# Conditioning products summed on VectorE, and RWKV's first pair with its inputs loaded at once

## The reference

```python
for l in range(DEPTH):                     # DEPTH = 2
    cond = jax.nn.silu(c) @ w_ada[l] + b_ada[l]
    shift, scale, gate_raw = jnp.split(cond, 3, axis=-1)
    h = x * (1.0 + scale[:, None]) + shift[:, None]
    proj = h @ w_in[l]
    ...
    a = jax.nn.sigmoid(rw_a0[l] + a_down @ rw_a_up[l])
    kk = heads(k * rw_k_k[l], RW_HEAD)
    kk = kk / jnp.maximum(jnp.sqrt(jnp.sum(jnp.square(kk), -1, keepdims=True)), L2_EPS)
    ...
    x = layer_norm(DN_ALPHA * x + (1.0 + gate_raw[:, None]) * out, ln_g[l], ln_b[l])
...
mod = silu_c @ w_ada[l] + b_ada[l]         # second model, 6 * 1024 wide
mod_c = silu_cc @ w_ada[l] + b_ada[l]      # the same weights, another vector
```

## Time and profile before

| | us |
|---|---|
| Median of 3 runs (lowest to highest) | 5123.26 (5112.72 to 5138.3) |
| Profiled execution, its time | 5130.85 |
| Its span, first to last instruction | 5129.1 |
| Mean granted clock of TensorE | 0.907 |
| Busy: TensorE, VectorE, ACT, GpSimd | 4337.1, 1568.6, 1108.3, 751.6 |
| Last operation of `modulation` starts | 62.16 |
| First projection matmul of layer 0 (L400) | 87.51 |
| Last copy of layer 0's projection (L340) | 608.63 |

### The profile page before, as it was taken

How to read it: one execution, slowest core, us unless ns; L and a number is a source line. 1 busy time by engine, 2 the same in 40 slices (tenths; PEclk the granted TensorE clock), 3 DMA queues, 4 the chain that set the end, 5 groups by cost and what they waited for, 6 DMA issues and landing times. The chain is left out here.

```text
span 5129.1 us, 74458 instructions
## 1 busy us (share of the span) xinstructions
PE 4337.1 (85%) x28872; PEld 2808.1 (55%) x28872; DVE 1568.6 (31%) x2365; ACT 1108.3 (22%) x1499; POOL 751.6 (15%) x555
## 2 busy tenths in 40 slices
PE   6999867887998899757779996888778999999962
PEld 3666655665665688646656664453434444444431
DVE  2000265443232100645542412452221111111127
ACT  1000233322122111333321213340201111111110
POOL 1111101001222322000102220000050000000014
PEclk8999977878999899878879998999779999999985
DMA  4334312231221222210002221000107999999966
...
DMA packets 170080, 715.25 MB, mean 139 GB/s; under 512 B 26882, under 2 KB 28675, under 8 KB 134019
## 3 DMA queue, kind: packets, MB, share of 16 engines
...
## 5 line engine op out<-in xcount | busy, mean ns | idle before, releaser
L400 PE MATMUL ps<-s_proj_hS,s_proj_wS 128*128 128x512 f32 x3216 | 762.3, 398 | 62.2 <-POOL s_proj_wS L312 62.2
L400 PEld LDWEIGHTS ps<-s_proj_hS,s_proj_wS 128*128 128x128 f32 x3216 | 605.6, 189 | 223.6 <-ACT s_proj_wS L361 63.1
L1806 PE MATMUL ps<-s_mix_hS,s_mix_wS 128*128 128x512 f32 x1536 | 394.9, 413 | 40.1 <-POOL s_mix_wS L1665 35.5
L1806 PEld LDWEIGHTS ps<-s_mix_hS,s_mix_wS 128*128 128x128 f32 x1536 | 291.4, 190 | 134.9 <-issue 67.5
L2720 PE MATMUL ps<-s_exp_gu,keep_hT 128*128 128x512 f32 x736 | 340.1, 605 | 14.8 <-DMA s_exp_gu<-in_w_gu_dram 12.9
L2704 PE MATMUL ps<-s_exp_wd,s_exp_aT 128*128 128x512 f32 x736 | 332.9, 595 | 1.9 <-ACT s_exp_aT L2630 1.9
L2725 PE MATMUL ps<-s_exp_gu,keep_hT 128*128 128x512 f32 x736 | 330.9, 592 | 0.0
L1665 POOL TENSOR_TENSOR s_mix_wS<-s_mix_w,s_mix_wS 128x1024 fp32r<-128x1024 f32 x96 | 230.7, 2404 | 582.3 <-ACT s_mix_wS L1674 582.3
L312 POOL TENSOR_TENSOR s_proj_wS<-s_proj_w,s_proj_wS 128x1024 fp32r<-128x1024 f32 x67 | 162.8, 2433 | 690.1 <-ACT s_proj_wS L361 690.0
L340 DVE COPY s_proj_o<-ps 128x512 f32<-128x512 f32 x66 | 45.6, 692 | 707.4 <-PE ps L400 707.4
L2670 DVE TENSOR_TENSOR s_exp_sg<-s_exp_sg,ps 128x256 f32<-128x256 f32 x92 | 38.7, 421 | 660.1 <-ACT s_exp_sg L2651 660.1
...
## 6 DMA issues: line engine op xcount, KB each, us to landing
...
```

Of the source, the lines that this page charges most:

```text
L400: mm = pe.matmul(k.ps[:, 6 + half if last else 2 * b + half, :], wS[:, b, x, t, :], hS[:, y, t, half * HALF:(half + 1) * HALF], start=(t = ...
L1806: mm = pe.matmul(k.ps[:, bank, :], wS[:, b, u, x, :], src[:, v, x, :], start=(x == 0 and u + v == 0), stop=(x == KT - 1 and u == 1))
```

## The change

`modulation` makes only slabs 0 to 15. Layer 0's gate joins the slabs that are made during layer 0's projection. These are made in another way: for 8 slabs at a time (a round of the projection), tiles that hold the c-th 128 inputs of all 8 slabs are loaded, c = 0 to 7, in four buffers within `k.mix`; VectorE multiplies each by one scalar per partition (`k.silu`) and adds it to a running sum, one sum for layers 0 and 1 (`ONE`, rounds 0 to 3), two for the second model (`TWO`, rounds 4 to 9). The tiles are worked in the first two steps of a round. At the head of the next round TensorE sums over the partitions: 8 matmuls for each sum, the sum as the stationary operand and one column of ones as the moving one. The products before were for three vectors in all slabs; now they are only for those that are used.

In `rwkv`, the first pair's key, query, low-rank weights come ahead of the masks, the masks have a semaphore of their own, decay, rate and norms go to banks 6, 4 and 2, and the three products stand one behind another.

```diff
     GRP = 4
-    NG = NADA1 // GRP
+    NS = 2 * KT
+    NG = NS // GRP
...
 
     nc, I = k.nc, k.I
     NB = 3
-    R1, R2 = 1, 9
-    NX = (2 * NADA1 + NADA2 - NADA1) // (NB * (R2 - R1))
+    ONE, TWO = (2 * KT, 4), (2 * NADA1, 6)
+    NWA = 4
...
+            acc, wa = k.mix[:, 0:2], k.mix[:, 2:2 + NWA]
+            ld_a = [s.sem(f"ld_a{x}") for x in range(NWA)]
+            acc_ready, ada_ready, ada_taken = [s.sem("acc_ready0"), s.sem("acc_ready1")], s.sem("ada_ready"), s.sem("ada_taken")
...
-            parts = [(0, 1, False), (1, 2, True), (2, R2, True), (R2, NR - 1, False), (NR - 1, NR, False)] if not l else \
-                [(0, 1, False), (1, NR - 1, False), (NR - 1, NR, False)]
-            for a, z, ada in parts:
-                if z == a + 1:
-                    for b in range(NB):
-                        yield a, b, ada
+            na, nb = ONE[1], ONE[1] + TWO[1]
+            parts = [(0, 1, ONE, None), (1, 2, ONE, ONE), (2, na, ONE, ONE), (na, na + 1, TWO, ONE), (na + 1, nb, TWO, TWO), (nb, NR, None, TWO)] if not l else \
+                [(0, 1, None, None), (1, NR - 1, None, None), (NR - 1, NR, None, None)]
...
-                            yield i, b, ada
+                            yield i, b, cur if b < 2 else None, old if b == 0 else None
...
+        def group(g, kind):
+
+            return (g - ONE[1], 2, TWO[0], range(1, 3)) if kind is TWO else (g, 1, ONE[0], range(0, 1))
...
-            for i, b, ada in steps(sp):
+            def tiles(i, b, cur):
+                g, nv, s0, vs = group(i, cur)
+                for c in range(4 * b, 4 * b + 4):
+                    wait(sp, acc_ready[0], i * KT + (c - NWA + 1))
+                    if nv == 2:
+                        wait(sp, acc_ready[1], g * KT + (c - NWA + 1))
+                    sp.dma_start(wa[:, c % NWA].rearrange("p (g n) -> p g n", g=KT),
+                                 I["w_ada"][bass.ds(g * KT + s0, KT), :, c, :].rearrange("g p n -> p g n")).then_inc(ld_a[c % NWA], 16)
+
+            late = []
+            for i, b, cur, old in steps(sp, unrolled=True):
                 n = i * NB + b
                 wait(sp, lo_ready, n - NB + 1)
                 src = I["v_down"] if isinstance(n, int) and n == NSCAN else I["w_in"][l, n]
                 sp.dma_start(w[:, b], src).then_inc(ld_w[b], 16)
-                if ada:
-                    m = n - R1 * NB
-                    wait(sp, ada_ready, m)
-                    for x in range(NX):
-                        sp.dma_start(wa[:, x], I["w_ada"][m * NX + (NADA1 + x)]).then_inc(ld_a[x], 16)
+                late.append((i, b, cur))
+                if len(late) > 2 and late[-3][2]:
+                    tiles(*late[-3])
...
                 wait(dve, st_o[b], i * 16, 16)
                 dve.tensor_copy(o[:, b, HALF:T], k.ps[:, 2 * b + 1, :]).then_inc(taken_v, 1)
-                m = n - R1 * NB
-                if ada and not (isinstance(m, int) and m == 0) or isinstance(n, int) and n == R2 * NB and not l:
-                    wait(dve, turned, m)
-                    dve.tensor_copy(k.cond[:, bass.ds((m - 1) * NX + NADA1, NX), :],
-                                    k.ps[:, 7, 0:3 * NX].rearrange("p (g v) -> p g v", g=NX)).then_inc(ada_taken, 1)
-                if ada:
-                    wait(dve, ada_ready, m + 1)
-                    dve.tensor_copy(row[:], k.ps[0:3, 6, 0:NX * P]).then_inc(row_ready, 1)
+                if old:
+                    g, nv, s0, vs = group(i - 1, old)
+                    wait(dve, ada_ready, i)
+                    dve.tensor_copy(k.cond[:, bass.ds(g * KT + s0, KT), vs[0]:vs[0] + nv],
+                                    k.ps[:, 7, 0:KT * nv].rearrange("p (v g) -> p g v", v=nv)).then_inc(ada_taken, 1)
+                if cur:
+                    g, nv, s0, vs = group(i, cur)
+                    for c in range(4 * b, 4 * b + 4):
+                        wait(dve, ld_a[c % NWA], i * 2 * 16 + (c // NWA + 1) * 16, 16)
+                        for v in range(nv):
+                            done, at = acc_ready[v], (g if v else i) * KT + c
+                            scale = k.silu[:, c, vs[v]:vs[v] + 1]
+                            if c:
+                                wait(dve, done, at)
+                                dve.scalar_tensor_tensor(acc[:, v], wa[:, c % NWA], scale, acc[:, v], ALU.mult, ALU.add).then_inc(done, 1)
+                            else:
+                                wait(dve, ada_ready, i)
+                                dve.tensor_scalar(acc[:, v], wa[:, 0], scale, None, ALU.mult).then_inc(done, 1)
...
-            for i, b, ada in steps(pe):
+            for i, b, cur, old in steps(pe):
                 n = i * NB + b
                 last = isinstance(n, int) and n == NSCAN
+                if old:
+                    g, nv, s0, vs = group(i - 1, old)
+                    wait(pe, acc_ready[0], i * KT)
+                    if nv == 2:
+                        wait(pe, acc_ready[1], g * KT + KT)
+                    wait(pe, ada_taken, i - 1)
+                    for v in range(nv):
+                        for x in range(KT):
+                            mm = pe.matmul(k.ps[:, 7, v * KT + x:v * KT + x + 1], acc[:, v, x * P:(x + 1) * P], k.ones[:, 0:1],
+                                           start=True, stop=True)
+                    mm.then_inc(ada_ready, 1)
                 wait(pe, hi_ready, n + 1)
                 wait(pe, lo_ready, n + 1)
...
         bones, lora, vup = s.sb("bones", [P, P]), s.sb("lora", [P, 2, P]), s.sb("vup", [32, 2, P])
         proj, vfirst = k.scratch["proj"], k.scratch["vfirst"]
 
+        def prep(q, x):
+
+            return 6 if q else {"decay": 6, "rate": 4, "residual": 2, "norms": 2}[x]
+
         def previous(n):
             return edge[:, n, 0:T]
 
...
+            sp.dma_start(par[:, :, 0:13], I["rw_par"][l]).then_inc(ld_par, 16)
             sp.dma_start(b, proj[CLOW]).then_inc(ld_low, 16)
-            sp.dma_start(par[:, :, 0:13], I["rw_par"][l]).then_inc(ld_par, 16)
+            sp.dma_start(e1, proj[CK]).then_inc(ld_k, 16)
+            sp.dma_start(lora[:, 0], I["rw_lora"][l, 0]).then_inc(ld_lora, 16)
+            if l:
+                sp.dma_start(vup[:, 0], I["v_up"][0]).then_inc(ld_lora, 16)
+            sp.dma_start(e2, proj[CR]).then_inc(ld_r, 16)
             sp.dma_start(pairs, I["pair_masks"][:, 0:1 + NLV, :]).then_inc(ld_pm, 16)
+            sp.wait_ge(low_in, 1)
+            sp.dma_start(b, proj[CV]).then_inc(ld_v, 16)
+            if l:
+                sp.dma_start(vf[:], vfirst[0]).then_inc(ld_vf, 16)
             for h in range(2):
-                sp.dma_start(mLN[rows(h)], I["causal_masks"][rows(h), :, rows(h)]).then_inc(ld_par, 16)
-                sp.dma_start(at_st[rows(h)], I["level_masks"][rows(h), 1:2 + NLV, rows(h)]).then_inc(ld_par, 16)
-            sp.wait_ge(low_in, 1)
-            inputs(0)
+                sp.dma_start(mLN[rows(h)], I["causal_masks"][rows(h), :, rows(h)]).then_inc(ld_mask, 16)
...
             act.activation(lo[0:HD, :], lo[0:HD, :], ACT.Tanh).then_inc(low_tanh, 1)
             key_part(0)
             query_part(0)
-            value_part(0)
             square(0)
             decay(0)
             rate(0)
+            value_part(0)
             residual(0)
             norm(0)
             exps(0)
...
-            dve.wait_ge(ld_par, 16 * NMASK)
+            dve.wait_ge(ld_par, 16)
...
+            dve.wait_ge(own, mine.n)
+
+            shift_key(0)
+            shift_query(0)
+            floor(0)
+            shift_value(0)
+            mix(0)
+            dve.wait_ge(shift_v, 1)
+            cumulate(0)
             for h in range(2):
                 dve.wait_ge(turn_m, 1)
                 mine.mark(dve.tensor_copy(at_ts[rows(h)], banks(k, 0)[rows(h), 0:(1 + NLV) * P]
                                           .rearrange("p (m n) -> p m n", n=P)[:, :, rows(h)]))
-            dve.wait_ge(own, mine.n)
-
-            shift_key(0)
-            shift_query(0)
-            shift_value(0)
-            floor(0)
-            mix(0)
-            dve.wait_ge(shift_v, 1)
-            cumulate(0)
...
+            dve.wait_ge(ld_mask, 16 * NMASK)
...
-                pe.wait_ge(ssm_ready, q + 1)
+                if q:
...
-                    pe.wait_ge(sig_a, q + 1)
...
-                pe.wait_ge(sig_w, q + 1)
+                wait(pe, sig_w, q + 1 if q else 0)
...
+            pe.wait_ge(low_tanh, 1)
+            pre_decay(0)
+            pre_rate(0)
+            key_norms(0)
             pe.wait_ge(ld_pm, 16)
             for n in range(1 + NLV):
                 tr = pe.transpose(banks(k, 0)[:, n * P:(n + 1) * P], pairs[:, n, :], k.eye[:])
             tr.then_inc(turn_m, 1)
-            pe.wait_ge(low_tanh, 1)
-            pre_decay(0)
-            key_norms(0)
-            pre_rate(0)
             pre_residual(0)
```

72 lines of the change are left out of this document (32 added, 40 removed).

## The result

The changed kernel took 4955.42 us (median of 4 runs, 4942.27 to 4966.35) where the kernel before took 5126.38 (4 runs, 5112.72 to 5138.3): ratio 0.9675, 95% interval 0.9654 to 0.9695. The forecast was 5000 with a range from 4962 to 5055. The profiled execution of the changed kernel took 4947.87 us (span 4946.1, mean granted clock 0.911), 183 us less than that of before.

A forecast was written before the change was run, and what follows sets the result against it. The prediction took TensorE alone to bound layer 0's projection. Its terms, -15.9 - 149.0 + 32.4 + 13.5 + 20 - 24 = -123 us, from the median of 5123.3 gave 5000 us, range 4962 to 5055.

The forecast's parts named there:

- VectorE's chain: Layer 0's projection, six two-sum rounds: TensorE waits 2.2 us each for VectorE's accumulations, slowed by GpSimd; +13.5 us.
- the pair loops: RWKV from the low-rank load of the second pair to merge, in both layers; forecast 0.
- What bounds the kernel: Layer 0's projection is TensorE alone; RWKV's first pair is a chain round ACT, TensorE, VectorE and the SP queue.
- modulation: Stage before the projection: layer 0's gate moved away, two of six groups go; -15.9 us.
- the removed work: Layer 0's projection: conditioning products and turning go from 24 steps, all on the path; -149.0 us.
- The narrow matmuls: Layer 0's projection: 128 one-column matmuls on TensorE at 0.253 us each, as the turning matmuls; +32.4 us.
- The clock: Layer 0's projection: waiting plus narrow matmuls drop TensorE to half clock in six rounds, 3.35 us each; +20 us.
- Tiles in 512-byte rows: Layer 0's projection: tile loads of 1024 runs of 512 bytes, 2.3 us a tile, hidden at no cost.
- RWKV's first pair: RWKV, both layers: earlier loads and back-to-back products bring the first unit operation forward; -24 us, between -16 and -27.
- Rival 1: Nothing lost on TensorE: GpSimd doesn't block or slack takes it, and the clock holds; -156 us, 4967; chance 0.20.
- Rivals 2 and 3: Projection's tile loads late: some gain left, 5030 to 5100, chance 0.15; or slower, 5149 and up, chance 0.05.
- Rival 4: RWKV's new order brings nothing, because of VectorE's mask copies or a late value slab; 5024; chance 0.08.

The follow-up runs named there:

- spread: Changed kernel with the one-column matmuls put one by one among the same step's projection matmuls instead of in a block at the head; 4932.80 us, ratio 0.9641.
- six_buffers: Changed kernel with six tile buffers instead of four, so SP leaves its tile loop earlier; 4972.73 us, ratio 0.9716.
- one_narrow: Changed kernel with one matmul of 8 or 16 columns replacing each head's one-column matmuls; projection 378.9 us, results not preserved.

## Why the prediction was wrong

Two steps failed: VectorE's chain was priced at 13.5 us and cost nothing, and the pair loops were put at nothing and gave some 24. The first made the forecast 13.5 us too slow within the range. The second took the time out of it: the fixed stretches alone, -147 us, would give 5126 - 147 = 4979 us, above the lower end of 4962.

**What bounds the kernel, modulation, the removed work.** Right. Modulation gave -15.8 us for -15.9. In the projection, -149.0 and what came in, 27.7 (narrow matmuls) + 14.1 (clock) + 0 (waiting) = 41.8, make -107.2, where -106.7 was measured. Its miss of 24 us is 13.5 (chain) + 5.9 (clock) + 4.7 (narrow matmuls).

**The narrow matmuls**, 32.4 us forecast: 4 x 1.70 + 6 x 3.49 = 27.7. The turning matmuls were the right row, at 0.253 a little dear against 0.218; spread shows 0.22 us even between other matmuls. By the rule of the Trainium skill ("VectorE: DVE Perf Modes", the TRN2 errata section) the estimate for 128 of them, two records each, was 6 us; the measured 27.7 us decides.

**VectorE's chain**, 13.5 us forecast, 0 measured: this step failed. "GpSimd makes one low half each step, 2.40 us, two of them inside the chain: 24.6 us." The block is real, 2.1 us each (2.40 taken), and with two of them TensorE does wait 1.5 to 1.6 us (six_buffers). But only one lay in the chain. Two paragraphs on I wrote that SP waits in the tile loop and holds back the next slab's load until "some 12 us into a round", and priced that at nothing for TensorE. I did not carry it to GpSimd, whose subtraction needs the same slab. The late load delays the operation that would have delayed the chain.

**The clock**, 20 us forecast, 14.1 measured, in the six rounds named. The cause named was narrow matmuls together with a wait ahead of them; the blocks of 16 did it with no wait (one_narrow and spread show that it is the block). 3.35 us was taken for each fall. Three came to 3.15 and three to 1.55, because there the block ran ahead of the fall and half clock lasted only some 3 us.

**Tiles in 512-byte rows**: hidden, as forecast, at an estimated 1.93 us a tile (2.3 taken, ends 1.38 and 3.2). VectorE waits for no tile. The Trainium skill has 207 or 103 GB/s for rows at a large pitch ("DMA: Bandwidth & Descriptors", Latency and other measured facts). There the large pitch lay between the partitions. Here neighbouring partitions' rows lie 4 KB apart and only the eight slabs 512 KB, and by the row above the tiles came to an estimated 271.

**RWKV's first pair**: -24 forecast, -10.4 - 14.3 = -24.7. Layer 0 gave 1 us less and layer 1 1.6 more. Decay and rate took 3.8 us together instead of 6.35, but ACT's tanh ended 9.1 us after the first load, not 8.2, and in layer 0 the unit operation waited for ACT's norm (1.74 us idle in the row above). ACT began the norm late because it stores layer 0's value slab first, and so waited 1.71 us for VectorE's value shift; two table loads of 1.28 us each, which the sum had not counted, lie in it too.

**What was not in the sum**: the pair loops. This is the other step that failed. Their code does not change, so they stood at nothing, without a look at what their clock does, and no end of the range allowed for it. In profiles they are 17 us shorter in layer 0 and 9 to 10 in layer 1 with the new projection, in layer 0 at a mean granted clock of 0.84 instead of 0.81. The medians point the same way: 171, 174 and 160 us for the whole change against 147 for its fixed stretches. With the projection's 24 us the 24 of the first measurement are the whole miss of 48. That the clock is higher is measured; why it is higher stays open, since neither the first pair nor the work or time ahead explains it. A range must hold it: two profiles of the same kernel differed by up to 14 us in this loop alone.

**Rivals.** Rival 1 (nothing lost on TensorE, 4967) came nearest by number, partly by luck: there was no wait, but the clock did not hold, and the pair loops made up for the clock. Rivals 2 and 3 (late tiles) had the wrong edge too: their excess 80t - 319 is zero at t = 4.0 us, not 4.4, and the four short rounds alone would be late from (35.6 - 8.3) / 8 = 3.4; at 1.93 it makes no difference. Rival 4 falls with the first pair's -24.7 us.
